# One decoder step on Trainium2: scale, shift, gate and norm-weight rows loaded once and spread by TensorE

## The reference

```python
for l in range(DEPTH):                                  # DEPTH = 2
    sp = adaln(c_prompt, w_ada[l], b_ada[l])            # six rows of 1024: one per sequence
    hp = modulate(rmsnorm(xp, norm_mix[l]), sp[0], sp[1])
    mp = mla_prompt(hp, ...) if l == 0 else pool_mixer(hp, ..., w_pool, pool_scale)
    xp = xp + sp[2][:, None, :] * mp
    hp = modulate(rmsnorm(xp, norm_ffn[l]), sp[3], sp[4])
    xp = xp + sp[5][:, None, :] * peer(hp, w_peer_q[l], peer_subkeys[l], peer_u[l], peer_v[l])
    ...                                                 # the same for the sample tokens

def modulate(h, shift, scale):
    return h * (1 + scale[:, None, :]) + shift[:, None, :]
```

## Time and profile before

| What | Value |
|---|---|
| median of 3 runs | 3487.39 us (3481.72 to 3490.45) |
| profiled execution, its own time | 3478.81 us |
| its span, first to last instruction | 3477.0 us |
| TensorE busy, mean granted clock | 80%, 0.883 |
| VectorE, ScalarE, GpSimd busy | 65%, 30%, 35% |
| DMA moved | 1266.40 MB, 364 GB/s over the span |
| gathers' queue, SyncE's queue | 1091.03 MB, 172.85 MB |

### The profile page before, as it was taken

The page is one execution under the profiler, slowest core; times in us unless marked ns, Lnnn a source line. Parts: engine busy times, 40 slices in busy tenths (PEclk is TensorE's granted clock), DMA queues, the critical chain, the costliest instruction groups (busy, mean ns, idle before and its releaser), DMA issues.

```text
span 3477.0 us, 39434 instructions
## 1 busy us (share of the span) xinstructions
PE 2769.2 (80%) x11227; PEld 1231.0 (35%) x11227; DVE 2276.8 (65%) x6373; ACT 1038.8 (30%) x4428; POOL 1211.8 (35%) x1077
## 2 busy tenths in 40 slices
PE   4988889979889957988989769979875775666765
PEld 0345554434444423434434234434331232112321
DVE  1454558887877856777777576777776645565455
ACT  0222224424334412433435314434421111111111
POOL 0000014433333423443434334434444344444443
PEclk9989999989999978999999979999988677777777
DMA  9650049999999998999999989999999999999998
GB/s 338 253 207 24 13 182 406 407 364 409 376 375 413 404 354 358 416 401 408 409 397 410 417 337 414 412 405 419 403 391 411 410 422 409 421 406 372 421 421 353
DMA packets 201876, 1266.40 MB, mean 364 GB/s; under 512 B 23762, under 2 KB 44803, under 8 KB 61874
## 3 DMA queue, kind: packets, MB, share of 16 engines
q0 software_dynamic: 150784, 1091.03, 76.9%
q1 hardware_dynamic: 50873, 172.85, 13.1%
HBM read 1260.46 MB, written 3.79 MB: 364 GB/s over the span
## 4 chain that ended last, share of the span: by engine, by line
PE 40%; DMA 29%; DVE 15%; issue 7%; ACT 3%; POOL 2%; SPq 1%; DVEq 0%; POOLq 0%; ACTq 0%; PEldq 0%
PE bank L1106 15%; DMA ring<-in_uv,work 10%; DMA big<-in_uv,work 8%; DMA mod_mix<-in_uv,work 7%; PE bank L844 6%; PE bank L956 5%; DVE ring L1946 2%; DMA ring<-in_w_ada 2%; PE bank L861 2%; PE bank L790 2%; ACT work L1425 1%; PE bank L660 1%; PE bank L617 1%; PE bank L691 1%; POOL ring L1464 1%
## 5 line engine op out<-in xcount | busy, mean ns | idle before, releaser
L1106 PE MATMUL bank<-ring,work 128*64 128x512 f32 (+1 forms) x2080 | 909.3, 710 | 276.6 <-ACT work L1425 276.2
L1464 POOL DMA_INDIRECT ring<-in_uv,work x520 | 608.8, 1171 | 944.5 <-PE bank L1106 818.8
L1946 DVE CUSTOM_DVE_ANT_0 ring<-ring,mod_smp 128x1024 f32<-128x1024 f32 x512 | 622.3, 1224 | 273.2 <-DMA ring<-in_uv,work 266.4
L1413 ACT ACTIVATE work<-work 128x2 f32<-128x2 f32 x520 | 105.2, 202 | 1509.9 <-DVE work L1946 1509.6
L1464 POOL DMA_INDIRECT big<-in_uv,work x260 | 299.6, 1152 | 682.8 <-PE bank L1106 367.9
L844 PE MATMUL bank<-big 128*128 128x512 f32 x1024 | 512.1, 623 | 0.0
L1106 PE MATMUL bank<-big,work 128*64 128x512 f32 (+1 forms) x1040 | 317.7, 730 | 152.8 <-ACT work L1425 152.6
L1106 PEld LDWEIGHTS bank<-ring,work 128*64 128x64 f32 (+1 forms) x2080 | 211.2, 153 | 627.7 <-ACT work L1425 387.5
L1946 DVE CUSTOM_DVE_ANT_0 big<-big,mod_smp 128x1024 f32<-128x1024 f32 x256 | 309.8, 1224 | 138.9 <-DMA big<-in_uv,work 135.0
L1106 PE MATMUL bank<-work 128*64 128x512 f32 (+1 forms) x520 | 293.8, 693 | 93.6 <-ACT work L1425 93.5
L1425 ACT ACTIVATE work<-small,work 128x64 f32<-128x64 f32 (+1 forms) x1040 | 303.2, 339 | 145.2 <-DVE work L1956 139.1
(11 more groups left out here) (289 smaller groups left out, 3404.2 us busy)
## 6 DMA issues: line engine op xcount, KB each, us to landing
big<-in_wk SPq DMA_DIRECT2D x48, 1152.0 KB, 10.1
ring<-in_w_ada SPq DMA_DIRECT2D x64, 768.0 KB
work<-in_cache_mla SPq DMA_DIRECT2D x104, 160.0 KB, 8.9
ring<-in_uv,work POOLq DMA_INDIRECT x520, 11.8
big<-in_uv,work POOLq DMA_INDIRECT x260, 12.1
ring<-in_w_mla_out SPq DMA_DIRECT2D x1, 4096.0 KB, 13.0
big<-in_w_mla_out SPq DMA_DIRECT2D x4, 1024.0 KB, 11.6
mod_smp<-in_cache_mla SPq DMA_DIRECT2D x24, 160.0 KB, 12.7
```

Source lines behind the costliest of these rows:

```text
L1106: last = mm(out, diag[:, t % 2, j, 0:min(m, HALF)], s[:, D + half * 512:D + (half + 1) * 512], start=(k == 0 and (n < S0 or j == 0)), stop ...
L1413: act.activation(acts[:, t % 2 * GRP:(t % 2 + 1) * GRP], dots[:, t % 2 * GRP:(t % 2 + 1) * GRP], ACT.Gelu)\
L1464: pool.indirect_dma_start(slot[g % SLOTS], None, T["uv"].rearrange("l e d -> (l e) d"), bass.IndirectOffsetOnAxis(index[:, k * GRP + j:k * ...
L1946: dve.tensor_tensor_reduce(u, u, hb, 1.0, 0.0, ALU.mult, ALU.add, dots[:, at:at + 1]).then_inc(sem("dots_set"), 1)
```

## The change

In the expert turns a row comes into partition 0 alone (4 KB). TensorE multiplies a column of ones by it, 512 columns at a time, into bank 0 or 1, and ScalarE copies the bank over all 128 partitions of the row's tile. That is 28 products and 28 copies. `row_at` says at which turn which row is spread: the three of t = 47 in halves at turns 51 to 56 through bank 0; four of each mixer opening at `mix_at - 1` to `mix_at + 2`, both halves in one turn; `pool_scale` at `mix_at + 4`; the gate in halves at `mix_at[6] + 11` and + 12. `rows_till(t)` counts the halves spread before turn t, and TensorE, ScalarE and VectorE wait for such counts. The gate's load moves from `mix_at[6] + 1` to + 8. Six semaphores go (`own_used`, `pool_gain_in`, `gate_in` and three of single weights: the loads of four weights share one now) and three come. The product stands first in TensorE's `background(t)`, the copy first in ScalarE's `late_background(t)`.

```diff
+        row_at = {51: (mod_ffn[:, 0, :], 0), 52: (mod_ffn[:, 0, :], 1), 53: (mod_ffn[:, 1, :], 0), 54: (mod_ffn[:, 1, :], 1),
+                  55: (gain, 0), 56: (gain, 1)}
+        for n_ in mix_at:
+            for i_, row_ in enumerate((mod_pool[:, 0, :], gain_pool, mod_pool[:, 1, :], mod_pool[:, 2, :])):
+                row_at[mix_at[n_] - 1 + i_] = (row_, None)
+            row_at[mix_at[n_] + 4] = (gain_pool, None)
+        row_at[mix_at[6] + 11] = (mod_ffn[:, 2, :], 0)
+        row_at[mix_at[6] + 12] = (mod_ffn[:, 2, :], 1)
...
+        def rows_till(t):
+            return sum(len(halves_of(k)) for k in row_at if k < t)
...
@@ SyncE, t == 47
-                        ld(mod_ffn[:, m, :], ada_rows[1, NC - 1, (3 + k) * D:(4 + k) * D].partition_broadcast(P), "mods_in")
-                    ld(gain, T["norm_ffn"][1].partition_broadcast(P), "mods_in")
+                        ld(mod_ffn[0:1, m, :], ada_rows[1, NC - 1:NC, (3 + k) * D:(4 + k) * D], "rows_in")
+                    ld(gain[0:1, :], T["norm_ffn"][1:2], "rows_in")
...
@@ SyncE, mix_at[n] - 2 and + 2
-                        mods(mod_pool, 1, 0, "prompt", P, T["norm_mix"][1], gain_pool)
+                        for m, k in ((0, 1), (1, 0), (2, 2)):
+                            ld(mod_pool[0:1, m, :], ada_rows[1, NC - 1:NC, k * D:(k + 1) * D], "rows_in")
+                        ld(gain_pool[0:1, :], T["norm_mix"][1:2], "rows_in")
                     if t == mix_at[n] + 2:
                         w.next("mods_set")
-                        ld(gain_pool, T["pool_scale"][0].partition_broadcast(P), "pool_gain_in")
+                        ld(gain_pool[0:1, :], T["pool_scale"][0:1], "rows_in")
...
-                if t == mix_at[6] + 1:
+                if t == mix_at[6] + 8:
                     sp.wait_ge(sem("x_routed"), NT)
-                    ld(mod_ffn[:, 2, :], ada_rows[1, NC - 1, 5 * D:6 * D].partition_broadcast(P), "gate_in")
+                    sp.wait_ge(sem("row_kept"), rows_till(mix_at[6] + 5))
+                    ld(mod_ffn[0:1, 2, :], ada_rows[1, NC - 1:NC, 5 * D:6 * D], "rows_in")
...
@@ TensorE, pool_map; the same kind of wait stands in queries and key_scores
+                if n in mix_at:
+                    pe.wait_ge(sem("row_kept"), rows_till(mix_at[n] + 5))
...
+            rows_given = {51: 3, mix_at[4] - 1: 7, mix_at[4] + 4: 8, mix_at[6] - 1: 12, mix_at[6] + 4: 13, mix_at[6] + 11: 14}
+
+            def spread_row(t):
+
+                row = row_at[t][0]
+                if t in rows_given:
+                    pe.wait_ge(sem("rows_in"), 16 * rows_given[t])
...
+                if rows_till(t):
+                    pe.wait_ge(sem("row_kept"), rows_till(t))
+                for half in halves_of(t):
+                    mm(pb[half if row_at[t][1] is None else 0][:, :], ones[0:1, :], row[0:1, half * 512:(half + 1) * 512], start=True, stop=True)\
+                        .then_inc(sem("row_ps"), 1)
+
             def background(t):
+                if t in row_at:
+                    spread_row(t)
...
@@ ScalarE
+            def keep_row(t):
+                row = row_at[t][0]
+                for i, half in enumerate(halves_of(t)):
+                    act.wait_ge(sem("row_ps"), rows_till(t) + i + 1)
+                    act.activation(row[:, half * 512:(half + 1) * 512], pb[half if row_at[t][1] is None else 0][:, :], ACT.Copy)\
+                        .then_inc(sem("row_kept"), 1)
+
             def late_background(t):
+                if t in row_at:
+                    keep_row(t)
...
@@ VectorE: set_mods, the multiply at mix_at + 5, mixer_hidden at mix_at + 2 and the routed result of tile 4 wait for counts of row_kept
-                        set_mods(mod_pool, P, gain_pool)
+                        set_mods(mod_pool, P, gain_pool, ("row_kept", rows_till(mix_at[n] + 1)))
...
-                        w.next("pool_gain_in", 16)
+                        dve.wait_ge(sem("row_kept"), rows_till(mix_at[n] + 5))
+                        dve.sem_inc(sem("link_done"), 1)
```

More of the change, by code:

```diff
@@ L330, in decoder_step, with halves_of @@
         assert out_turn + 10 < smp_open[S0], out_turn
+        row_at = {51: (mod_ffn[:, 0, :], 0), 52: (mod_ffn[:, 0, :], 1), 53: (mod_ffn[:, 1, :], 0), 54: (mod_ffn[:, 1, :], 1),
[6 more added lines that the diff above has]
+        row_at[mix_at[6] + 12] = (mod_ffn[:, 2, :], 1)
+        def halves_of(t):
+            return (0, 1) if row_at[t][1] is None else (row_at[t][1],)
+        def rows_till(t):
+            return sum(len(halves_of(k)) for k in row_at if k < t)
         page_at = {page_turn[k]: k for k in page_turn}
@@ L435, in _ @@
             load_mix_w(3)
-            ld(w_ukT, T["w_ukT"], "mix_w_in4")
+            ld(w_ukT, T["w_ukT"], "mix_w_in1")
             ada_slices(2 * NSLICE, 2 * NSLICE + ADA_SLOTS)
@@ L686, in project @@
                 if i == 0:
-                    for k in range(1, 5):
-                        w.next(f"mix_w_in{k}", 16)
+                    w.next("mix_w_in1", 16, 4)
                 for b in range(3):
@@ L954, in queries @@
                         pe.wait_ge(sem("qT_ready"), i)
+                    if rows_till(head_turn(q, h) - 6):
+                        pe.wait_ge(sem("row_kept"), rows_till(head_turn(q, h) - 6))
                 for c in range(DC):
@@ L966, in key_scores @@
                     pe.wait_ge(sem("sco_ready"), i)
+                if rows_till(head_turn(q, h) - 3):
+                    pe.wait_ge(sem("row_kept"), rows_till(head_turn(q, h) - 3))
                 if choices_till(head_turn(q, h) - 2):
@@ L1032, in spread_choice @@
                 last.then_inc(sem("choice_ps"), 1)
+            rows_given = {51: 3, mix_at[4] - 1: 7, mix_at[4] + 4: 8, mix_at[6] - 1: 12, mix_at[6] + 4: 13, mix_at[6] + 11: 14}
[3 more added lines that the diff above has]
+                    pe.wait_ge(sem("rows_in"), 16 * rows_given[t])
+                if t == 51:
+                    pe.wait_ge(sem("qT_ready"), PH + 1)
+                for n in mix_at:
+                    if t == mix_at[n] - 1:
+                        pe.wait_ge(sem("qT_ready"), n // 2 * PH)
+                        pe.wait_ge(sem("expert_set"), n // 2 * 2 * PH)
+                if t == mix_at[6] + 11:
+                    pe.wait_ge(sem("x_pooled"), NT)
+                if rows_till(t):
[3 more added lines that the diff above has]
+                        .then_inc(sem("row_ps"), 1)
             def background(t):
+                if t in row_at:
+                    spread_row(t)
                 for n in norm_turn:
@@ L1491, in set_mods @@
             def set_mods(m, n, gain_=hT, loads=("mods_in", 16, 4)):
-                w.next(*loads)
-                d(stt(m[0:n, 0, :], m[0:n, 0, :], 1.0, gain_[0:n, :], ALU.add, ALU.mult), "mods_set" if loads[0] == "mods_in" else "smp_mods_set")
+                if loads[0] == "row_kept":
+                    dve.wait_ge(sem("row_kept"), loads[1])
+                    dve.sem_inc(sem("link_done"), 1)
+                else:
+                    w.next(*loads)
+                d(stt(m[0:n, 0, :], m[0:n, 0, :], 1.0, gain_[0:n, :], ALU.add, ALU.mult), "smp_mods_set" if loads[0] == "smp_mods_in" else "mods_set")
             def norm(xt, hb, m, n):
@@ L1846, in routed @@
                 if n == NT:
-                    w.next("gate_in", 16)
+                    dve.wait_ge(sem("row_kept"), rows_till(mix_at[6] + 13))
+                    dve.sem_inc(sem("link_done"), 1)
                 add_rows(t, (mod_row if n >= S0 else mod_ffn)[:, 2, :], "x_routed", ybank(i))
@@ L1907, in background @@
                 if t == 70:
[L1908 removed]
+                    set_mods(mod_ffn, P, gain, ("row_kept", rows_till(57)))
                 for r in range(NS):
```

10 lines of the change are left out of this document (6 added, 4 removed).

## The result

The changed kernel takes 3496.74 us (median of 6 runs, 3490.92 to 3501.4) against 3483.34 us (6 runs) for the kernel before, measured side by side: ratio 1.0042, 95% interval 1.0029 to 1.0054. It is 13.4 us slower, where the prediction had no change as the likeliest.

The account below looks back on a forecast made before the run. Neither TensorE nor DMA alone was taken as the bound: saved bytes count before the openings, the order of waits at them. Terms -1 (layer 1), +3 (first opening), -5 and +3 (second) sum to 0: 3487 us, range 3468 to 3504.

Parts of the forecast that it names:

- The bytes of the second opening: Just before 1918 us, four broadcast loads fewer where DMA is full: -5.0 us.
- The first opening: From turn 127, TensorE waits for the row instead of VectorE at turn 129: net +1 to +6 us, taken as +3.
- late row: Rival, first opening: row lands when the pages did, 1281.6 to 1283 us, TensorE resumes 15 us later; 3502 us, chance 0.13.
- The pooling scale is issued at 2035.14 us as before, behind the pages.: Second opening: scale's issue time unchanged, its row landing at about 2039 us, with TensorE waiting at turn 260.
- the same term: Second opening's wait for the pooling scale, moved to TensorE at turn 260: +3 us, between -5 and +8.
- The other term: Layer 1's expert rows, 811 to 880 us: 5.9 us of products less 3.95 idle and 3.8 of bytes, taken as -1.
- The prediction's own sign: Layer 1's rows: the prediction is wrong if 811 to 880 us grows by over 3 us.
- TensorE becomes the bound: Rival: products fall where TensorE is full, 5.9 us at layer 1's rows, 4 more behind each opening; 3502 us, chance 0.11.
- each slower case: Whole kernel slower by over 0.3%: "late row" 0.13 and "TensorE becomes the bound" 0.11, each +15 us; together 0.24.
- the 3 to 5 us more: Second opening: extra wait of the row if an engine drains a whole packet before turning to the other queue; 3492 us.

Follow-up runs that it names:

- the scale ahead: Changed kernel with only the second opening's pooling scale row loaded ahead of the 16 pages instead of behind: 3485.11 us, ratio 1.0005 to the kernel before.
- the spreads early: Changed kernel with the second opening's four rows spread at turns 246 to 249 instead of 255 to 258: 3497.45 us, ratio 1.0032 to the kernel before.

## Why the prediction was wrong

**Right.** The products cost what the nearest rows gave: 1.95 to 1.98 us for two at full clock, 3.78 us at half (1.12 us for one by itself at full clock). In all they took 37.2 us, between the 27.7 and 53 us of the prediction. The copies cost 0.60 us and are hidden. The bytes of the second opening gave 4.7 us (predicted 5.0), and undone they were gone. The first opening went as told, link by link: TensorE standing at turn 127 (20.16 us, predicted 18 to 22), the gather queue dry, the rows in at 1270.6 us, where 1268 us and the 5.0 us that the kernel was behind by then make 1273. It lost 4.0 us (predicted +3, between +1 and +6); other executions of the same opening gave 0.9 to 4.4. The "late row" rival is out.

**The step that failed: "The pooling scale is issued at 2035.14 us as before, behind the pages."** It was issued 6.4 us later than being 8.2 us behind explains. I had put the spreads of turns 255 to 258 "in time" and looked only at when their rows arrive, not at what stands behind their products on TensorE: the context product, and behind that SyncE's page loads and the scale. Two spreads, 6.1 us, and a half-clock turn go straight into it; in three more executions the pages were later still, 10 us behind their place in the kernel before. This is the very question that I had asked of VectorE and ScalarE at the first opening and left out for SyncE at the second. The remainder of the same term was mis-sized: with the pages on time the opening still lost 7.3 us, not 3. I priced the wait by TensorE's own work behind it, 12.8 us, less its 8.94 us of idle time, and not by what stops with it: while TensorE stands no slot comes free, and DMA had nothing to move for 17 us of turns 258 to 272 where it was 8 us before. With the scale ahead it was 9 us and the step +0.1. The term came to +10.3 to +13.5 in four executions, where +3 was taken and +8 was the upper end.

**The other term: layer 1's rows, taken as -1, measured +2.9 (to +4.4 in other executions).** The bytes gave 3.0 us (predicted 3.8). The products cost 5.8 of 5.9 us: the 3.95 us of idle time that I subtracted were not to be had. The window of the earlier trace rows is full in the changed kernel (68.99 of 69 us busy), but the idle time came back in the turns behind it, and over turns 51 to 64 it was 9.9 us before and 8.9 after. The prediction's own sign, that this stretch grows by over 3 us, came true. Doubling the products settled it. The "TensorE becomes the bound" rival had this term right; its 4 us more behind each opening were not there at the first, and at the second the loss came of late pages and an empty DMA, not of the products' own time.

**Sum.** By steps: -3.0 + 5.8 + 4.0 - 4.7 + 11.3 = +13.4, against a predicted -1 + 3 - 5 + 3 = 0. Of the difference some 4 us are layer 1's, 8 us the second opening's, 1 us the first's. The range (3468 to 3504) holds the time, but for another reason than the forecast's. The chance of slower, 0.24, was too low, since each slower case was priced alone, while here a piece of one of them and a loss that none of them named fell together.

**The queue.** The row of the second opening landed 3.1 us after its issue (2049.71 to 2052.86), with the spreads early 3.8 us (2040.31 to 2044.14); I had taken 3.9. The Trainium skill ("DMA: Bandwidth & Descriptors", Queues, rings and completion order) has an engine drain a packet of some 9 to 17 descriptors before it turns to the other queue; the 3 to 5 us more that I had worked out from this did not come. But these rows don't test it: between the row's issue and its landing the loads' queue moved 810 packets and the gathers' queue one, so there was no other queue to turn from. The 827 against 849 packets of the earlier trace rows don't speak against it either, as the prediction has it: turns of any equal length give equal counts over 17 us. Where the gathers do compete, with the rows ahead of the pages at the first opening, a wait of that size is seen, though not whether it comes of this rule. The three rows were issued at 1244.02 us and the fourth at 1244.88 us, and from 1244 to 1247.4 us DMA moved only packets of gathers:

```profile
q0 software_dynamic: 193, 1.44, 100.8%
```

At the second opening of the same kernel, with DMA empty, the row issued at 2000.50 us was through by 2001.6 us (the prediction took 1.5 us for this, without a row):

```profile
q1 hardware_dynamic: 2, 0.00, 1.1%
```

A sentence of the same section, that a row may land before the whole queue is through, can't be told from these rows.

## What to carry to other kernels

Before moving work onto an engine, list what is queued behind it there and which loads those instructions release; two spreads of 2 to 4 us ahead of the product that frees the page buffers delayed 16 pages and all that follows them. Price a wait by what stops with it: an engine that stands and frees no buffers leaves DMA empty, and that time was not made good here. Idle time summed over a window is not cover: double the added work in an experiment and see whether the turns grow one for one. And where a small load is stuck behind large ones, its place in the queue decides, not its size: the same reordering gave 13 to 16 us with 512 KB broadcasts as well, while making the loads 128 times smaller and leaving them in their place made the kernel 13 us slower, for the 8 us of bytes that it saved.

## What the runs showed of the hardware

- A float32 product of one partition by 512 columns cost what one of 128 partitions does: 587 ns at the least for a pass, 1219 ns at half clock. Behind each stall of 14 to 20 us for a row TensorE's first products ran at the lower level, 1.2 GHz (3.78 us for four passes against 1.95); the granted clock of 2050 to 2060 us was 0.52.
- Beside a standing TensorE the loads' queue moved 2444 packets in 17 us, where in competition with the gathers it moved 849.
- The issue of 13 pages on SyncE took 14.2 us with four 4 KB rows in front, 21.2 us with 2.1 MB and 35.2 us with 4.2 MB in front of them: what is ahead in a queue is paid in the issuing engine's time too.
- Beside competing gathers a 4 KB row had moved nothing 3.4 us after its issue; on an empty DMA one was through in 1.1 us.
- The same passes of TensorE took 14.71 us at a granted clock of 0.50 and 9.65 us at 0.78, in two kernels that have the same TensorE instructions there.
